# A hybrid decoder step on one core: the prompt's mixer split as 256 and 768 tokens in place of 512 and 512

## The reference

```python
hn = rmsnorm(x, norm1_w) * (1.0 + sc1) + sh1            # sc, sh, g: from mod = silu(c) @ w_ada + b_ada
q, k, v, g_ret, x_lru, g_lru, gate_a, gate_b = split(hn @ w_in)
o, S = retention(rope(q), rope(k) / 8, v, S0)           # 8 heads, 64 keys, 128 values, chunks of 128
xl = causal_conv(x_lru)                                 # 4 taps
a = exp(-8 softplus(-lam) * sigmoid(xl @ wa + ba))      # block-diagonal
h = scan(a, sqrt(1 - a * a) * sigmoid(xl @ wx + bx) * xl)
merged = sigmoid(gate_a) * silu(g_ret) * groupnorm(o) + sigmoid(gate_b) * h * gelu(g_lru)
x = x + g1 * (merged @ w_out)
hn2 = rmsnorm(x, norm2_w) * (1.0 + sc2) + sh2
for 8 heads: s1, s2 = query halves @ 128 keys each; top 16 of each; top 16 of the sums -> 16 experts of 16384
dots = gelu(hn2 . peer_u[expert]) * softmax(scores)     # 128 experts per token
x = x + g2 * sum(dots * peer_v[expert]);  y = rmsnorm(x, final_norm_w)
```

## Time and profile before

| | |
|---|---|
| median of 3 runs | 4320.67 us |
| profiled execution | 4329.52 us, span 4327.7 us |
| mean granted TensorE clock | 0.935 of 2.4 GHz |
| TensorE matmul busy | 3778.1 us, 87% |
| VectorE busy | 2810.0 us, 65% |
| GpSimd busy | 1689.8 us, 39% |
| ScalarE busy | 1558.0 us, 36% |
| transfers | 245 GB/s over the span |

### The profile page before, as it was taken

How to read it: one execution, slowest core, us unless ns; L and a number is a source line. 1 busy time by engine, 2 the same in 40 slices (tenths; PEclk the granted TensorE clock), 3 DMA queues, 4 the chain that set the end, 5 groups by cost and what they waited for, 6 DMA issues and landing times.

```text
span 4327.7 us, 66078 instructions
## 1 busy us (share of the span) xinstructions
PE 3778.1 (87%) x21008; PEld 2963.4 (68%) x21008; DVE 2810.0 (65%) x6512; ACT 1558.0 (36%) x3682; POOL 1689.8 (39%) x1320
## 2 busy tenths in 40 slices
PE   8999999789988978945778888999889999999998
PEld 4666666576444547834567767787778888788887
DVE  2333333355787786658888888898887888775100
ACT  3112111111222221187344444555455555555400
POOL 0000000024334334516665566666665777563000
PEclk9999999899999998956989999999999999999999
DMA  6222221347666667717988888999899999997444
GB/s 212 67 67 92 66 80 43 138 135 243 223 220 226 225 229 281 266 55 265 347 319 309 325 309 333 360 348 361 341 370 372 380 380 386 373 366 268 135 151 137
DMA packets 416129, 1060.32 MB, mean 245 GB/s; under 512 B 39664, under 2 KB 169328, under 8 KB 415984
## 3 DMA queue, kind: packets, MB, share of 16 engines
q0 software_dynamic: 168000, 610.87, 38.0%
q1 hardware_dynamic: 242928, 437.39, 28.9%
q10 hardware_dynamic: 5056, 10.49, 0.7%
HBM read 1032.00 MB, written 26.62 MB: 245 GB/s over the span
## 4 chain that ended last, share of the span: by engine, by line
PE 35%; DVE 18%; DMA 13%; issue 9%; POOL 5%; ACT 1%; PEld 1%; ACTq 0%; POOLq 0%; DVEq 0%; SPq 0%; PEldq 0%
PE vacc L1872 14%; DMA rows<-in_peer_u,eidx 11%; DVE rows L1443 9%; PE vacc L707 6%; PE scat L1810 6%; POOL rows L1265 3%; PE vacc L676 2%; PE vacc L1784 2%; POOL hot L1256 2%; DMA vbuf<-in_peer_v 2%; DVE oh1w L1498 1%; DVE hot L1431 1%; DVE oh L1494 1%; PE scat L1859 1%; PE tps L1822 1%
## 5 line engine op out<-in xcount | busy, mean ns | idle before, releaser
L1872 PE MATMUL vacc<-W,vbuf 128*128 (+1 forms) x8192 | 1941.3, 393 | 32.2 <-DMA vbuf<-in_peer_v 20.9
L1872 PEld LDWEIGHTS vacc<-W,vbuf 128*128 128x128 f32 x8192 | 1566.0, 196 | 242.9 <-issue 33.9
L1265 POOL DMA_INDIRECT rows<-in_peer_u,eidx x1088 | 1329.6, 1222 | 918.4 <-DVE dots L1443 533.8
L1443 DVE CUSTOM_DVE_ANT_0 rows<-rows,htok 128x1024 f32<-128x1024 f32 x1088 | 1353.6, 1266 | 260.3 <-DMA rows<-in_peer_u,eidx 248.1
L1673 ACT ACTIVATE dist<-iota,e2s 128x128 bf16<-128x128 f32 x2048 | 649.0, 390 | 21.5 <-DVE wpart L1478 19.6
L1256 POOL TENSOR_TENSOR hot<-hot,cid 128x864 f32<-128x864 f32 x68 | 148.5, 2183 | 1294.0 <-DVE hot L1431 1293.5
L1680 ACT ACTIVATE W<-scat 128x256 f32 (+1 forms) x512 | 195.6, 382 | 973.3 <-PE scat L1859 906.0
L1859 PE MATMUL scat<-oh1w,oh 128*128 128x64 bf16 x6144 | 290.2, 199 | 244.8 <-DVE oh1w L1498 160.8
L1859 PEld LDWEIGHTS scat<-oh1w,oh 128*128 128x128 bf16 x6144 | 262.0, 101 | 338.3 <-issue 182.5
L1676 ACT ACTIVATE oh<-dist,ones 128x512 bf16<-128x512 bf16 x512 | 369.5, 722 | 16.7
L707 PE MATMUL vacc<-rows,W 128*128 128x288 f32 x1280 | 339.6, 421 | 20.6 <-ACTq L614 18.3
(11 more groups left out here) (272 smaller groups left out, 2834.5 us busy)
## 6 DMA issues: line engine op xcount, KB each, us to landing
vbuf<-in_peer_v SPq DMA_DIRECT2D x512, 512.0 KB
W<-in_w_in SPq DMA_DIRECT2D x80, 512.0 KB, 4.0
W<-in_wq SPq DMA_DIRECT2D x64, 512.0 KB
rows<-in_peer_u,eidx POOLq DMA_INDIRECT x1088
W<-in_w_in SPq DMA_DIRECT2D x16, 1024.0 KB
vbuf<-in_w_ada SPq DMA_DIRECT2D x8, 2048.0 KB, 8.1
W<-in_w_ada SPq DMA_DIRECT2D x4, 2048.0 KB, 19.4
W<-in_w_out SPq DMA_DIRECT2D x2, 4096.0 KB, 16.2
```

The costliest lines, as they stand in the source:

```text
L1265: g.indirect_dma_start(rows[:, s, :], None, table[:, :], bass.IndirectOffsetOnAxis(ap=eidx[:, (t // 2) % 2, t % 2, col:col + 1], axis=0)). ...
L1443: v.tensor_tensor_reduce(rows[:, s, :], rows[:, s, :], htok[:, t % 2, :], 1.0, 0.0, ALU.mult, ALU.add, dots[t % 2][:, c:c + 1]).then_inc(u ...
L1872: mm = pe.matmul(vacc[:, k, :], vbuf[:, s, k * P:(k + 1) * P], W[:, e1, :].rearrange("p o t -> p (o t)"), start=(clear and s == 0 and k % ...
```

## The change

- The mixer parts are 256 prompt tokens with the samples (320 columns, one slice, 2 + 1 tiles) and 768 prompt tokens (two slices of 384, 6 tiles). The retention stages of `zB` run in two quads of 4 and 2 chunks; the order of `mix_tensor` is rearranged, and `zB` calls `fill()` 14 times a turn. Some of its tiles move to `scr`, `x3`, `sqb` and to the room behind the weights.
- The samples go with group 0. One crossing stands before `zB`, three behind it; buffers of odd groups lie where `hnB` was.
- 316 dots and 16 units stand before the first scatter, 256 and 14 before. `dots` has three buffers. The 36 units now have other places; products of a unit are placed by `product_at`.
- GpSimd's folding addition is gone; VectorE reduces all 54 candidates.

```diff
-XG = ((0, GT), (GT, GT + TS), (2 * GT + TS, GT), (3 * GT + TS, GT))
+XG = ((0, GT + TS), (GT + TS, GT), (2 * GT + TS, GT), (3 * GT + TS, GT))
-LINKS = 18
+LINKS = 16
-SLOTS = 9
-ORDER = (0, 1, 2, 3, 8, 4, 5, 6, 7)
+SLOTS = 14
+ORDER = (0, 1, 8, 2, 3, 4, 5, 6, 7)
...
-    rows = [("p", 0, 0, 0, 4, 4), ("y", 0, 24, 4, 7, 24), ("m", 24, 112, 7, 9, SLOTS * H // 2),
-            ("n", 112, 200, 9, 10, SLOTS * H // 2), ("z", 200, 2 * P, 10, 14, 56)]
-    cuts = [2 * P, 2 * P, 2 * P + 32, 3 * P] + [3 * P + 64 * (i + 1) for i in range(11)] + [NU + 64, NU + 64]
-    units = [14, 15, 16, 18, 21, 24, 26, 28, 30, 32, 33, 34, 35, 36, 36, 36, 36]
+    rows = [("p", 0, 0, 0, 4, 4), ("y", 0, 12, 4, 5, 12), ("m", 12, 112, 5, 8, SLOTS * H // 2),
+            ("n", 112, 236, 8, 8, SLOTS * H // 2), ("z", 236, 2 * P, 8, 8, 20), ("r", 2 * P, 2 * P, 8, 11, 24),
+            ("s", 2 * P, 284, 11, 14, 28), ("t", 284, 316, 14, 16, 32)]
+    cuts = [316, 316, 340, 400] + [400 + (1024 - 400) * (i + 1) // 10 for i in range(10)] + [NU, NU + 64, NU + 64]
+    units = [16, 17, 18, 20, 22, 24, 26, 28, 30, 32, 33, 34, 35, 36, 36, 36, 36]
...
+        self.n = FIRST if sample else LATER
+        self.nt = self.n // P
+        self.quads = ((0, 2),) if sample else ((0, 4), (4, 6))
+        self.slices = ((0, TA),) if sample else ((0, CUT), (CUT, LATER))
...
             part(2, "pk", 0)
-            transposes(0)
-            part(2, "pk", 1)
+            for quad in z.quads:
+                transposes(0, quad)
...
+                part(2, "pk", 1)
+                for quad in z.quads:
+                    transposes(1, quad)
+                part(3, "pj", 0)
+                kv(z.quads[0])
+                part(3, "pj", 1)
+                kv(z.quads[1])
+                score(z.quads[0])
+                part(4, "pk", 0)
+                score(z.quads[1])
+                part(4, "pk", 1)
...
             dl_(v.tensor_tensor(z.ig, z.ig, z.xl, ALU.mult))
+            fill()
...
+            fill()
+            dl_(v.tensor_tensor(z.glru[:, 0:z.n], z.glru[:, 0:z.n], z.lh[:, z.lead:z.lead + z.n], ALU.mult))
...
-                    half = NCAND // 2
-                    gl_(g.tensor_tensor(hot[:, t, :, :], hot[:, t, :, :], bc(cid[:, t, :], 1, [P, TOPK, NCAND]), ALU.mult))
-                    g.tensor_tensor(hot[:, t, :, 0:half], hot[:, t, :, 0:half], hot[:, t, :, half:], ALU.add).then_inc(hot_ready, 1)
+                    g.tensor_tensor(hot[:, t, :, :], hot[:, t, :, :], bc(cid[:, t, :], 1, [P, TOPK, NCAND]), ALU.mult).then_inc(hot_ready, 1)
...
+                def product_at(m, x):
+
+                    G, h, _ = unit(m)
+                    at = min(done[m] + 3, (done + [NU])[m + 1] + 1) if x else done[m] + 1
+                    return min(at, G * GT + h * TOPK - 1)
...
-                    v.tensor_reduce(eidf[:, 0:nt, :], hot[:, 0:nt, :, 0:NCAND // 2], AX, ALU.add).then_inc(dk, 1)
+                    v.tensor_reduce(eidf[:, 0:nt, :], hot[:, 0:nt, :, :], AX, ALU.add).then_inc(dk, 1)
...
-                        if p == 8 and m:
+                        if p == 8 and m and m != H:
                             ids(m - 1)
...
+                    if half:
+                        ids(H - 1)
...
+                for g in range(1, NGRP + 1):
+                    for at in steps(plan[3 + g]):
+                        mixed_step(at)
+                    if g < NGRP:
+                        residual(g)
+                        scale(g)
...
+                x_load(1)
+                for j in range(16, 20):
+                    wq_load(j)
                 x_load(2)
```

More of the change, by code:

```diff
@@ L290, in program @@
         ef = sb(ctx, "ef", [P, 2, P])
-        dots = [sb(ctx, f"dots{u}", [P, P]) for u in range(2)]
+        dots = [sb(ctx, f"dots{u}", [P, P]) for u in range(3)]
         sel = ef[:, 0, 0:TS]
@@ L838, in mix_tensor @@
                 slab_turn()
+            part(5, "pk", 0)
+            if z.sample:
                 kv_s(4)
-            pe.wait_ge(xl_ready, f + (b + 1))
-            pe.wait_ge(wab_in, f * 32 + (32 * b + 32))
-            lru_gate(0)
-            part(5, "pk", 0)
-            outp()
+            for quad in z.quads:
+                outp(quad)
             part(5, "pk", 1)
@@ L972, in mix_vector @@
             v.wait_ge(mg_out, f * 16 + (16 * b + 16))
-            r = stage()
-            ins = v.tensor_copy(z.osb[:, 0:HALF], r[:, :])
+            for lo, hi in z.quads:
+                r = stage()
+                ins = v.tensor_copy(z.osb[:, lo * P:hi * P], r[:, 0:(hi - lo) * P])
+                if hi < z.nt or z.sample:
+                    ins.then_inc(st_free, 1)
+                if hi < z.nt:
+                    fill()
             if z.sample:
-                ins.then_inc(st_free, 1)
                 r = stage()
-                ins = v.tensor_copy(z.osb[:, HALF:TA], r[:, 0:TS])
+                ins = v.tensor_copy(z.osb[:, FIRST:TA], r[:, 0:TS])
             ins.then_inc(o_ready, 1)
@@ L1188, in _ @@
                     wq_load(j)
-                x_load(1)
                 x2_store(0)
-                for j in range(4, 20):
-                    wq_load(j)
-                x2_store(1)
                 for j in range(6):
@@ L1197, in _ @@
                 wab_load(sp, 0)
[L1198 removed]
+                for j in range(4, 16):
                     wq_load(j)
[L1200 to L1202 removed]
+                sp.wait_ge(q_ps, 16)
+                sp.wait_ge(tr_ready, 3)
+                sp.wait_ge(s_ps, H + NSU)
+                sp.wait_ge(x2_out, 16)
                 carry_load(sp, 0)
@@ L1442, in dot @@
                     v.wait_ge(landed[s], 16 * (n // VD + 1))
-                    v.tensor_tensor_reduce(rows[:, s, :], rows[:, s, :], htok[:, t % 2, :], 1.0, 0.0, ALU.mult, ALU.add, dots[t % 2][:, c:c + 1]).then_inc(used, 1)
+                    v.tensor_tensor_reduce(rows[:, s, :], rows[:, s, :], htok[:, t % 2, :], 1.0, 0.0, ALU.mult, ALU.add, dots[t % 3][:, c:c + 1]).then_inc(used, 1)
                 def vrow(n):
@@ L1451, in vrow @@
                     v.wait_ge(landed[s], 16 * (n // VD + 1))
-                    v.scalar_tensor_tensor(acc[:, :], rows[:, s, :], dots[0][:, c:c + 1], acc[:, :], ALU.mult, ALU.add).then_inc(used, 1)
+                    v.scalar_tensor_tensor(acc[:, :], rows[:, s, :], dots[(NT - 1) % 3][:, c:c + 1], acc[:, :], ALU.mult, ALU.add).then_inc(used, 1)
                 def tile_weights(t, n):
@@ L1557, in _ @@
                 tile_picks(1)
-                for row in plan[5:]:
+                for row in plan[8:]:
                     i = row[0]
@@ L1920, in _ @@
                 mix_tensor(pe, zB, H - 1, True)
-                cross(2)
-                cross(3)
+                for g in range(1, NGRP):
+                    cross(g)
                 pe.wait_ge(s_ready, NUNIT)
```

332 lines of the change are left out of this document (166 added, 166 removed).

## The result

The kernel after takes 4190.33 us (median of 4 runs, 4187.5 to 4194.2), the kernel before 4321.9 in the same comparison. The ratio is 0.9693, 95% interval 0.9678 to 0.9709: 132 us faster. The profiled execution has a span of 4188.7 against 4327.7 before, 139 less, and that is the sum to account for.

What follows compares the result with a forecast made beforehand. The prediction took TensorE to bound both mixer parts and VectorE the earlier quarters. It summed +83 us up to the first scatter and -145 behind it to -62, median 4259 us, range 4195 to 4325.

Steps and rivals of the forecast that it cites:

- First mixer part: Eight turns at 576 columns cut to 320: a turn falls from 89 to near 60 us, -232 in all.
- Rival (4): First mixer part doesn't shrink with its columns: turns of 66 us instead of 60, total 4307; chance 0.10.
- Crossing ahead of the second part: One crossing, with the samples, in place of two (113 + 148 us) before the second mixer part: -104 us.
- Second mixer part: 512 to 768 columns: +272 us for eight turns, +6 for dry moments, +14 for the tail behind the last turn.
- TensorE alone: +32.5: Second-part turn: parts +18, tiles +7, small matmuls +7.5; VectorE's loop 98 against 96 us adds 1.5, giving +34 a turn.
- dry moments: Second mixer part: indices of heads 6 and 7 come late, so two more moments without rows for VectorE, +6 us.
- Tail and crossings behind: After the second mixer part: a third crossing +110 us, and +17 for VectorE's dots and units beside the crossings.
- Quarters: Scatter and seven quarters after it: fewer dots and no folding addition, quarters about 140 us; 139 saved, -142 with the scatter.
- (2): Quarters fall to TensorE's floor: seven quarters take 133 us each, total 4210; chance 0.17.
- (3): The 96-dot quarter was held by gathers: first three quarters stay near 150 us, +30, total 4289; chance 0.10.
- (1): Second mixer part falls to VectorE's loop: from 110 us a turn the change is worth nothing, 116 gives 4371; chance 0.13.
- side estimate: Dots beside GpSimd's products: the folding addition's share would be 20 us, 6 within the seven quarters; left out of the sum.

Runs made afterwards that it cites:

- a_short: Kernel after, but the 224 dots in the second mixer part's slots multiply only 64 of 1024 elements, so output differs from the reference's: 4156.4 us, one run.
- a_long: Kernel after, with another VectorE operation over 1024 elements ahead of each of the 224 dots in the second mixer part's slots: 4302.55 us, one run.
- g_only: Kernel after with the earlier kernel's plan of dots and units and its folding addition, so only the new column split: 4317.04 us against 4325.68, ratio 0.998.
- a_prod: Kernel after with GpSimd's two products of a unit issued 6 and 8 dots behind its end, not 1 and 3: 4128.64 us, ratio 0.9547 to the kernel before.
- b_prod: Kernel before, folding addition kept, with the two products issued 6 and 8 dots behind a unit's end, not 1 and 3: 4225.16 us against 4325.68, ratio 0.9773.
- b_nofold: Kernel before without the folding addition, VectorE reducing all 54 candidates: 4292.39 us against 4325.94, ratio 0.9925.

## Why the forecast was right in kind and wrong in size

*First mixer part: nearly right.* Turns of 58.1 to 61.2 us where 60 was said, -243 for -232. Rival (4), 66 us a turn, is refuted.

*Crossing ahead of the second part: right*, -100 for -104.

*Second mixer part: the step that failed*, +239 for +292. The failing line is "TensorE alone: +32.5 ... So I add 1.5: +34 a turn, +272", with the two terms beside it. The seven whole turns grew by 28.4 (68.6 to 97.0), not 34: 2.8 of the 5.6 are the mis-sized small matmuls (4.7 for 7.5), 1.5 the charge for a VectorE loop believed equal, 1.3 that the average stood 3.6 over an undisturbed turn before and only 2.3 after. Over seven turns that is 39 us. The dry moments were charged at +6, which had the sign wrong: there was one late turn in place of two, with 4.3 us of TensorE's waiting in place of 13.7, and that gain is inside the 1.3. The last turn with its tail grew by 33 where 34 + 14 was said: 15. Against that, 7 came at the first projection, which the forecast had left out. The mechanism, TensorE's pace with VectorE just under it, was right, and `a_short` and `a_long` show it. Two sums of that line don't come out as written: five times 11.0 - 7.13 is 19, not 18 (18 is what 10.7 gives, and what was measured), and 65.0 + 32.5 is 97.5, not the 96 that the text holds against 98.

*Tail and crossings behind:* +120 for +127, of which the geometry alone is +101 (`g_only`); the dots and units add 19 where 17 was said.

*Quarters: right.* -141 for -139. Reduction without folding: 1.94 us (forecast 2.0). One thing in it was left open by the text, what a unit's wait is worth. The forecast priced a unit at 20 us, 7 of them idle, and took 2 off. `a_prod` and `b_prod` show that most of the idle part could have been had by moving two instructions. Rivals (2) and (3) are refuted for this kernel, as (1) is by turns of 97: the quarters stood at 140 on average, not 133, and the first at 142, not 150.

*From the eighth quarter:* -9 for -3, small and not taken apart.

The page "SBUF — State Buffer" of the Trainium skill (section "Who interferes with whom") has a VectorE instruction with two SBUF inputs contend with a GpSimd instruction that reads SBUF. The forecast's side estimate, set beside that page, was 20 us less in the dots without the addition (its 6 for the seven quarters should be about 9, as they hold 480 of the 1088 dots). The trace agrees in size: the mean dot fell from 1266 to 1247 ns, 21 us over 1088; in `b_nofold` it fell to 1254, 13 us. Which share of that reached the span was not separated from the shorter stall. And in `a_prod` the mean dot rose to 1272 ns, 27 us more over all dots, while the kernel became 62 us faster. Slower dots beside the products cost less than rows that are asked for late.

*The error as a whole.* The terms that failed were small, many and of one sign: each doubtful microsecond of the second part was charged, and eight turns multiply it. Its lower end for the part was +245 without the 20 for dry moments and the tail; the measured 239 has everything in it. The range should have been laid out by the turn, not by the sum. It was also narrower than its own ends: +30 before the scatter and -190 behind it add to -160, and the range stopped 126 under the kernel before.

## What to carry to other kernels

GpSimd works through its queue in order here, so a product that waits 7 us for its input holds up every request for rows behind it. Where an engine both computes and asks for transfers, issue its computing some steps after its input is surely there. Here that alone gave 101 us of 4326 (8 of them in front of the place where it can act), three quarters of what the whole restructuring gave. When a stage is repeated, take the difference of one undisturbed turn from instruction counts and multiply it; charges for possible waits belong in the range.

## What the runs showed of the hardware beyond that

The granted clock moves a TensorE-bound turn by 5%. Two turns of the first part in the kernel after, as windows, with equal work, and then the stretch that only the first of them has:

```profile
136.00:197.00 61.00, 55.70 (x212) 36.02 (x212) 21.85 (x52) 13.38 (x22) 0.00 (x0) 0.92 0.36 108
380.00:438.00 58.00, 52.66 (x212) 34.10 (x212) 21.84 (x52) 13.39 (x23) 0.00 (x0) 0.97 0.37 113
```

```profile
177.60:184.40 6.80, 6.42 (x19) 4.91 (x19) 2.18 (x3) 3.14 (x6) 0.00 (x0) 0.50 0.15 21
```

At a mean granted clock of 0.92 the turn is 61.2 us, at 0.97 it is 58.1, 212 matmuls in each. Both turns have a shorter stretch at the lower level (1.2 GHz); the first also has the one shown, at a clock of 0.50. In the 6.6 us ahead of it TensorE was busy for 6.2 and the clock stood at the upper level. How many of the seven measured turns are long differs from run to run: four take 61 us in the kernel after, none in `a_prod` (57.8 to 59.8), and that moves everything behind by 10 us. So stage marks of single profiles are good to that.

A product of GpSimd took 2.75 to 2.78 us at 22 of its 68 executions in the kernel after, and mostly 1.85 to 1.88 otherwise. What differs is a dot of VectorE that has just begun. The product of 2578.03 above (2.75 us, to 2580.78) and VectorE's two dots beside it:

```profile
2577.87 1.22 DVE L1479 CUSTOM_DVE_ANT_0 rows<-rows,htok 128x1024 f32<-128x1024 f32 x1
2579.01 2.86 DVE L1479 CUSTOM_DVE_ANT_0 rows<-rows,htok 128x1024 f32<-128x1024 f32 x1
```

All 22 long products begin 0.16 to 0.17 us behind the start of a dot of normal length, and end 1.70 to 1.73 us behind its end. The second dot here ends 1.09 us behind the product. So each seems to get hardly any of its work done while the other runs. The wait ahead of a product is not the cause: four products of `a_prod` that waited over 1 us took 1.85 to 1.87.
